# Attention of a fused transformer block, issued by pairs of heads: half-array scores and half-array value products

## The reference, cut to what matters

```python
# layer 0, for each block of 128 queries (12 heads of 64; top keys chosen by an indexer)
s = jnp.einsum('bthd,btkd->bthk', qi, k_sel) * HEAD_DIM ** -0.5
p = masked_softmax(s, valid[:, :, None, :])
out = jnp.einsum('bthk,btkd->bthd', p, v_sel)
# layer 1: three branches (31 compressed keys, selected keys, window), summed with gates
o = gi[..., 0:1] * o_c + gi[..., 1:2] * o_s + gi[..., 2:3] * o_w
# both layers: four more heads over 256 memory keys
s = jnp.einsum('bshd,bnhd->bhsn', q, k) * HEAD_DIM ** -0.5
p = jax.nn.softmax(s, axis=-1)
o = jnp.einsum('bhsn,bnhd->bshd', p, v)
```

## Time and profile before

| what | us |
|---|---|
| median of 3 runs (3523.74 to 3528.39) | 3527.47 |
| the profiled execution's own time | 3527.51 |
| its span in the trace | 3525.7 |
| layer 0's attention, in the trace | 208.6 to 299.3 |
| layer 1's attention, in the trace | 857.8 to 1060.7 |

### The profile page before, as it was taken

How to read it: one execution, slowest core, us unless ns; L and a number is a source line. 1 busy time by engine, 2 the same in 40 slices (tenths; PEclk the granted TensorE clock), 3 DMA queues, 4 the chain that set the end, 5 groups by cost and what they waited for, 6 DMA issues and landing times.

```text
span 3525.7 us, 46614 instructions
## 1 busy us (share of the span) xinstructions
PE 3348.1 (95%) x16902; PEld 2768.0 (79%) x16902; DVE 1657.1 (47%) x2719; ACT 1472.4 (42%) x2771; POOL 1601.7 (45%) x1404
## 2 busy tenths in 40 slices
PE   6899999999999999999989996899999999999998
PEld 4578888877778888788877775788888878888886
DVE  4784433142773332343326876555565552333321
ACT  3355433223664333333325554454445542243322
POOL 4245544662445445544553321444444435464454
PEclk8899999997999999999999997999999999999999
DMA  4111333341002333333332220111111113333332
GB/s 122 42 43 49 95 95 97 94 115 37 1 1 84 95 95 94 95 98 95 94 86 62 59 54 25 37 43 37 42 37 37 39 46 96 96 96 95 98 96 70
DMA packets 471315, 245.93 MB, mean 70 GB/s; under 512 B 13820, under 2 KB 468711, under 8 KB 471015
## 3 DMA queue, kind: packets, MB, share of 16 engines
q1 hardware_dynamic: 470144, 241.33, 24.1%
q10 hardware_dynamic: 998, 2.30, 0.2%
HBM read 241.51 MB, written 2.10 MB: 69 GB/s over the span
## 4 chain that ended last, share of the span: by engine, by line
PE 85%; DVE 8%; ACT 3%; issue 2%; POOL 1%; DMA 0%; ACTq 0%; DVEq 0%; POOLq 0%
PE ps L463 18%; PE ps L464 18%; PE ps L465 18%; PE ps L1545 3%; PE ps L1525 3%; PE ps L2281 2%; PE ps L2177 2%; PE ps L2179 2%; PE ps L2178 2%; PE ps L2263 2%; PE ps L1534 2%; PE ps L1696 1%; PE ps L1697 1%; PE ps L1698 1%; PE ps L1769 1%
## 5 line engine op out<-in xcount | busy, mean ns | idle before, releaser
L445 POOL TENSOR_TENSOR w_lo<-ring,w_hi 128x512 fp32r<-128x512 f32 (+1 forms) x908 | 1223.8, 1369 | 1540.6 <-ACT w_hi L436 1540.6
L436 ACT ACTIVATE w_hi<-ring 128x512 fp32r<-128x512 f32 (+1 forms) x908 | 516.1, 617 | 1276.5 <-PE ps L465 1191.8
L463 PE MATMUL ps<-h_hi,w_hi 128*128 128x512 f32 x1776 | 701.7, 395 | 4.4 <-POOL w_lo L445 4.4
L465 PE MATMUL ps<-h_hi,w_lo 128*128 128x512 f32 x1776 | 691.9, 390 | 0.0
L464 PE MATMUL ps<-h_lo,w_hi 128*128 128x512 f32 x1640 | 638.8, 390 | 0.0
L463 PEld LDWEIGHTS ps<-h_hi,w_hi 128*128 128x128 f32 x1776 | 333.8, 188 | 80.7 <-POOL w_lo L445 6.4
L465 PEld LDWEIGHTS ps<-h_hi,w_lo 128*128 128x128 f32 x1776 | 333.7, 188 | 69.8
L464 PEld LDWEIGHTS ps<-h_lo,w_hi 128*128 128x128 f32 x1640 | 308.4, 188 | 68.5 <-issue 5.0
L464 PE MATMUL ps<-a_lo,w_hi 128*128 128x512 f32 x752 | 292.5, 389 | 0.0
L465 PE MATMUL ps<-a_hi,w_lo 128*128 128x512 f32 x720 | 280.1, 389 | 0.0
L463 PE MATMUL ps<-a_hi,w_hi 128*128 128x512 f32 x720 | 280.1, 389 | 0.0
(11 more groups left out here) (445 smaller groups left out, 6195.1 us busy)
## 6 DMA issues: line engine op xcount, KB each, us to landing
ring<-in_ffn_w_in SPq DMA_DIRECT2D x176, 512.0 KB, 3.8
ring<-in_w_in SPq DMA_DIRECT2D x96, 512.0 KB, 4.0
ring<-in_ffn_w_down SPq DMA_DIRECT2D x32, 512.0 KB, 3.7
ring<-in_ffn_w_out SPq DMA_DIRECT2D x32, 512.0 KB, 3.6
ring<-in_w_o SPq DMA_DIRECT2D x16, 512.0 KB, 3.7
ring<-in_w_branch_gdn SPq DMA_DIRECT2D x16, 512.0 KB, 3.6
ring<-in_nsa_w_in SPq DMA_DIRECT2D x15, 512.0 KB, 3.8
ring<-in_dsa_w_in SPq DMA_DIRECT2D x13, 512.0 KB, 4.1
```

The costliest lines, as they stand in the source:

```text
L436: act.activation(w_hi[:, (halves(u) + j) % PIECES, 0:n, :], slot(u)[:, j * n:(j + 1) * n, :], ACT.Copy) \
L445: pool.tensor_tensor(w_lo[:, q % PIECES, 0:n, :], slot(u)[:, j * n:(j + 1) * n, :], w_hi[:, q % PIECES, 0:n, :].bitcast(f32), ALU.subtract ...
L463: pe.matmul(dst, wh, hi(k), start=first and k == 0, stop=False)
L465: ins = pe.matmul(dst, wl, hi(k), start=False, stop=last and k == 2 * n - 1)
```

## The change

Units are issued two at a time, the two heads of a pair for one query tile and branch (in layer 1 the order becomes tile, branch, head instead of tile, head, branch). The scores contract only the head's own 64 rows, and the value products have 64 weight columns and write only the head's own 64 output partitions, the two heads taking turns for each 128 keys. Each head now has an accumulation of its own. The loops of PE and ACT run over pairs of units: in step i PE issues the scores of both units of pair i, all transposes of pair i-2 and the value products of pair i-3, and ACT both exps of pair i and both evictions of pair i-2. The depths of all buffers and the count of instructions stay.

```diff
-    LEAD = 2
...
-            for t in range(NT):
-                for hh in range(2):
+            for t, br, hh in itertools.product(range(NT), range(1 if i == 0 else 3), range(2)):
...
-                        at = HD * (1 - hh)
+                        at = HD
                         us.append(dict(q=q_rot[:, pair, tok], k=k_dsa[:, hh, 0:nk], bias=bias, nk=nk,
-                                       v=[v_dsa[:, j, at:at + P] for j in range(t + 1)], gate=None, clamp=False,
-                                       out=tok, first=hh == 0, last=hh == 1, pair=pair, need=t))
+                                       v=[v_dsa[:, j, at:at + HD] for j in range(t + 1)], gate=None, clamp=False,
+                                       out=tok, first=True, last=True, pair=pair, need=t))
...
-        for n in range(N + LEAD + LAG_V):
-            if n < N:
-                u = us[n]
-                if n >= 4:
-                    pe.wait_ge(sig("att_masked").sem, t["masked"] + n - 3)
-                pe.matmul(ps[:, SCORE_BANKS[n % 4], 0:u["nk"]], u["q"], u["k"], start=True, stop=True) \
-                  .then_inc(sig("att_scores").sem, 1)
...
+        for i in range(N // 2 + LAG_V):
+            if i < N // 2:
+                if i >= 2:
+                    pe.wait_ge(sig("att_masked").sem, t["masked"] + 2 * i - 2)
+                for n in (2 * i, 2 * i + 1):
+                    u, rows_ = us[n], even_odd[n % 2]
+                    pe.matmul(ps[:, SCORE_BANKS[n % 4], 0:u["nk"]], u["q"][rows_], u["k"][rows_], start=True, stop=True) \
+                      .then_inc(sig("att_scores").sem, 1)
+            s = i - LAG_T
+            if 0 <= s < N // 2:
+                for m in (2 * s, 2 * s + 1):
+                    u = us[m]
+                    pe.wait_ge(sig("att_norm").sem, t["norm"] + m + 1)
+                    if m >= 2:
+                        pe.wait_ge(sig("att_copied").sem, t["copied"] + m - 1)
+                    for at, w in key_tiles(u):
+                        ins = pe.transpose(ps[0:w, 2 + m % 2, at:at + P], pr[:, m % DEEP, at:at + w], ident)
+                    ins.then_inc(sig("att_turned").sem, 1)
+            s = i - LAG_V
+            if 0 <= s < N // 2:
+                pe.wait_ge(sig("att_copied").sem, t["copied"] + 2 * s + 2)
...
                 for j, (at, w) in enumerate(tiles):
-                    ins = pe.matmul(ps[:, 4 + u["pair"] % 2, tok], u["v"][j], prT[0:w, m % 2, at:at + P],
-                                    start=u["first"] and j == 0, stop=u["last"] and j == len(tiles) - 1)
-                ins.then_inc(sig("att_value").sem, 1)
+                    for hh in range(2):
+                        u = us[2 * s + hh]
+                        ins = pe.matmul(ps[even_odd[hh], 4 + u["pair"] % 2, tok], u["v"][j], prT[0:w, hh, at:at + P],
+                                        start=u["first"] and j == 0, stop=u["last"] and j == len(tiles) - 1,
+                                        skip_group_check=True)
...
-            m = n - LAG_V - 2
+            m = n - 2 * LAG_V - 4
...
+        for i in range(N // 2 + LAG_V + 1):
+            if i < N // 2:
+                for n in (2 * i, 2 * i + 1):
+                    u = us[n]
+                    act.wait_ge(sig("att_max").sem, t["max"] + n + 1)
+                    if n >= DEEP:
+                        act.wait_ge(sig("att_turned").sem, t["turned"] + n - DEEP + 1)
...
+            s = i - LAG_T
+            if 0 <= s < N // 2:
+                for m in (2 * s, 2 * s + 1):
+                    u = us[m]
+                    act.wait_ge(sig("att_turned").sem, t["turned"] + m + 1)
+                    if m >= 2:
+                        act.wait_ge(sig("att_value").sem, t["value"] + m - 1)
```

More of the change, by code:

```diff
@@ L8 @@
 import numpy as np
+import itertools
 from concourse import mybir
@@ L1476, in units_of_layer @@
                     g = h // (TOK_HEADS // 2)
[L1477 to L1487, removed]
+                    at = HD * (2 * g + 1)
+                    u = dict(gate=gates[:, t, 3 * h + br:3 * h + br + 1], out=tok, first=br == 0,
+                             last=br == 2, pair=pair, clamp=br == 0, need=0)
+                    if br == 0:
+                        u |= dict(q=q_raw[:, pair, tok], k=k_cmp[:, g, hh, 0:NC], bias=cmp_bias[:, t, 0:NC],
+                                  nk=NC, v=[v_cmp[0:NC, at:at + HD]])
+                    else:
+                        u |= dict(q=q_rot[:, pair, tok], k=k_pad[:, br - 1, g, hh, 0:nk], bias=cb, nk=nk,
+                                  v=[v_tok[:, br - 1, j, at:at + HD] for j in range(t + 1)])
+                    us.append(u)
         for pair in range(MEM_PAIRS):
@@ L1491, in units_of_layer @@
                     tok = slice(t * P, (t + 1) * P)
-                    at = HD * hh
+                    at = 2 * HD * hh
                     us.append(dict(q=q_mem[:, pair, tok], k=k_mem[:, pair, hh, :], bias=const("causal")[:, 0:N_MEM],
-                                   nk=N_MEM, v=[v_mem[:, j, pair, at:at + P] for j in range(MT)], gate=None,
-                                   clamp=False, out=tok, first=hh == 0, last=hh == 1, pair=PAIRS + pair, need=0))
+                                   nk=N_MEM, v=[v_mem[:, j, pair, at:at + HD] for j in range(MT)], gate=None,
+                                   clamp=False, out=tok, first=True, last=True, pair=PAIRS + pair, need=0))
         return us
@@ L1519, in pe_attention @@
         pe.wait_ge(sig("pads_zero").sem, (1, 4)[layer])
-        for n in range(N + LEAD + LAG_V):
-            if n < N:
-                u = us[n]
-                if n >= 4:
-                    pe.wait_ge(sig("att_masked").sem, t["masked"] + n - 3)
-                pe.matmul(ps[:, SCORE_BANKS[n % 4], 0:u["nk"]], u["q"], u["k"], start=True, stop=True) \
-                  .then_inc(sig("att_scores").sem, 1)
[L1527 to L1540, removed]
+        for i in range(N // 2 + LAG_V):
[19 more added lines that the diff above has]
+                pe.wait_ge(sig("att_copied").sem, t["copied"] + 2 * s + 2)
+                u = us[2 * s]
+                if u["pair"] >= 2 and (s == 0 or us[2 * s - 1]["pair"] != u["pair"]):
@@ L1544, in pe_attention @@
                 for j, (at, w) in enumerate(tiles):
[L1545 to L1547 removed]
+                    for hh in range(2):
[3 more added lines that the diff above has]
+                                        skip_group_check=True)
+                        if j == len(tiles) - 1:
+                            ins.then_inc(sig("att_value").sem, 1)
     def dve_attention(dve, ch, t):
@@ L1551, in dve_attention @@
         need = 0
-        for n in range(len(us) + LAG_V + 3):
+        for n in range(len(us) + 2 * LAG_V + 5):
             if n < len(us):
@@ L1590, in act_attention @@
         N = len(us)
[L1591 to L1611, removed]
+        for i in range(N // 2 + LAG_V + 1):
[5 more added lines that the diff above has]
+                        act.wait_ge(sig("att_turned").sem, t["turned"] + n - DEEP + 1)
+                    act.activation(pr[:, n % DEEP, 0:u["nk"]], sm[:, n % DEEP, 0:u["nk"]], ACT.Exp,
+                                   bias=neg_max[:, n % 8:n % 8 + 1], accum_out=row_sum[:, n % 8:n % 8 + 1]) \
+                       .then_inc(sig("att_prob").sem, 1)
+            s = i - LAG_T
[5 more added lines that the diff above has]
+                        act.wait_ge(sig("att_value").sem, t["value"] + m - 1)
+                    w = min(P, u["nk"])
+                    n_t = len(key_tiles(u)) * P
+                    act.activation(prT[0:w, m % 2, 0:n_t], ps[0:w, 2 + m % 2, 0:n_t], ACT.Copy) \
+                       .then_inc(sig("att_copied").sem, 1)
+            m = 2 * (i - LAG_V) - 1
+            if 0 < m < N and (m == N - 1 or us[m + 1]["pair"] != us[m]["pair"]):
```

## The result

The changed kernel takes 3583.86 us (median of 4 runs, 3579.71 to 3592.85) against 3527.93 for the kernel before (4 runs on the same chip): ratio 1.0167, 95% interval 1.0153 to 1.0181. It is slower by 56 us. The forecast was slower by 21.5.

The account below looks back on a forecast made before the run. PE's own issue was taken to bound attention before, a chain through DVE and ACT after. From 3527.5 us, -8 at the full clock and +30 for clock falls gave 3549; own case 3535 to 3565, 8-in-10 range 3516 to 3585.

Parts of the forecast that it names:

- Halves side by side: PE's products on separate array halves overlap: scores fall from 0.43n to 0.21n us per pair-step, value products taken as 0.21n.
- Rival 3: Value products on column halves don't overlap, so hops grow by 0.21c, +27 us: 3566 us; chance 0.15.
- 0.55 us of drains in a pair-step: PE changes array shape three times per pair-step, draining each time: 0.2 + 0.2 + 0.15 us.
- The chain through the second exp and the evictions: From V(i-4) to V(i-2), through scores, both DVE units, second exp, evictions, transposes, values: 1.92 + 0.84a + 0.11b + 0.43c us.
- rival 2: The chain is looser than read and engines' sums decide: 9.5 and 26 us per pair of heads, 3490 us; chance 0.04.
- rival 1: The clock holds in attention, since PE never pauses more than some 3 us: -8, 3519 us, faster; chance 0.15.
- rival 4: The clock stays at 1.2 GHz through attention, PE's sums at half speed, +80 us: 3607 us; chance 0.08.
- rival 5: The clock costs are twice too high and the rest right: 3534 us and below, no measurable change; chance 0.12.
- Both chains have six hops and sizes that add up to 12: ... 28.1: Layer 1's twelve pair-steps per period: 28.1 us against 29.98, -1.9 per pair of heads, -11.4 over six.
- In layer 1 the small steps fall each time, and 3 us ... doubles: +18: Clock falls over layer 1's four small steps each period, doubling 3 us of the chain's PE work: +18 us.
- Layer 0's clock, +5: In layer 0 two of three periods see a clock fall, doubling 1.2 us of PE work: 6 x 0.8 = +5 us.
- The starts: Ramp and tail, one more DVE unit at either end of two layers: +2 us; layer 1's start at half clock: +4.

Follow-up runs that it names:

- half_scores_old_order: The kernel before with only its scores changed to contract the head's own 64 rows, units still issued one by one: 3633.85 us, ratio 1.0294.
- evict_first: The changed kernel with ACT's two evictions of pair i-2 put ahead of its two exps of pair i in each step: 3516.80 us, ratio 0.9971.
- full_scores: The changed kernel with the old scores over all 128 rows, half-array value products kept: 3552.34 us, ratio 1.0077 to the kernel before.

## Why the prediction was right in sign and off in size

- **Halves side by side**: right, for columns too (0.06 us a record). Rival 3 is refuted, though its 3566 was nearer to the time than the forecast.
- **0.55 us of drains in a pair-step**: about right in the sum. The hops of layer 0 at the full clock came out at 5.47 and 6.57 with 5.45 and 6.49 forecast, and the memory step at 2.36 with 2.35 (9.42/4). A single change cost 0.11 to 0.13 us in half_scores_old_order, after what the removed pauses gave, where the sum has 0.15 to 0.2.
- **The chain through the second exp and the evictions**: right, and shown by evict_first and the three like it. It is why PE's saved time didn't show (rival 2 falls with it; rival 1 falls by PEclk, 0.89 and 0.80; rival 4, the clock at half throughout, by PEclk too; rival 5, 3534, by the time). What I held against rival 4, that full stretches bring the clock back, isn't safe either: half_scores_old_order stood at half for 54.5 us with PE busy throughout.
- **"Both chains have six hops and sizes that add up to 12: ... 28.1"**: wrong. I took two chains that don't touch. They share DVE. In layer 0 the even sizes are always the late ones, and the sum holds. In layer 1 equal sizes follow each other, and the path through both chains, as the rows of full_scores have it, is longer than either. full_scores shows 31.5 at the full clock, 1.5 to 2.7 above what was expected of it; the changed kernel's own value, by the slope, is near 30.5. So layer 1 had about nothing to gain even at the full clock (29.98 before): some 2.4 us per pair of heads, 14 us in all, are missing in the forecast.
- **"In layer 1 the small steps fall each time, and 3 us ... doubles: +18"**: the sign right, the size off by about two. Three falls in a period, not one. The mean period of 37.1 us is 6.6 above the 30.5 of the slope and 5.6 above full_scores' period without a fall: 34 to 40 us over six pairs of heads, so 16 to 22 are missing here. I had looked for long pauses only; the falls above stand behind pauses of 1.1 to 1.9 us. I had also counted half-array scores only as PE time saved. With full ones in their place, in the same chain, the time at half clock is 34 us, not 129, and in the old order they brought a fall with no pause in PE's row.
- **Layer 0's clock, +5**: right in its periods (12.9 measured; 11.94 + 0.8 forecast). **The starts**: the first copy comes 8.7 us later in layer 0 and 8.4 in layer 1, of which 2.3 come back between the last token copy and the last memory copy. That makes some 15 us, where the forecast had some 10 for starts, ramps and memory steps.

From copy to copy, layer 1's five periods give +34 where the forecast had 5.5, and that is 28.6 of the 34.5 us by which it missed. The step that failed is thus layer 1's, in two terms, chain and clock. They may feed each other: a slower clock makes the chain's PE work longer, and a longer chain leaves PE more pauses; that the pauses pull the clock is argued, since the half-array scores go with the falls as well. How much is whose stays open within 1 us per period, since no run had the changed kernel's own layer 1 free of falls.

## What to carry to other kernels

Before halving an engine's work, find what it will then wait for. Grouping steps in twos put a second exp between a transpose and its eviction, and cost 50 us; with ACT's two blocks exchanged, the changed kernel's instructions were 0.3% faster than the kernel before. When two chains alternate on the same engines, sum the longest path through both, not each alone: they are independent only if one is always the late one. And TensorE's saved time isn't always free: look at the granted clock, and keep the full-array form where the saving lies off the path (here the scores) and the half-array form only where it lies on it (here the values).

## What the runs showed of the hardware

- Value products on separate column halves of the array, two heads in turn, start every 0.054 us at the full clock, half of the 0.11 of full ones. This is from the changed kernel's layer 0, where 8, 12 and 16 records took 0.59, 0.80 and 1.02 us to the next start (from 245.94, 248.32 and 250.97).
- A change between 64-row scores and full-array work cost 0.11 to 0.13 us each in half_scores_old_order's stream without pauses, after what the removed pauses gave.
- In the changed kernel's layer 1 the clock fell behind stretches in which PE was busy for 38, 44 and 66%, with pauses of 1.1 to 1.9 us in them. Full-array scores in the same chain took the time at half clock in attention from 129 to 34 us.
- It also fell without a pause: in half_scores_old_order PE's row was busy for 150.0 of 150.0 us at the full clock and then for 54.5 of 54.5 at half. With full scores the same order of work shows no such fall. What in the half-array scores does it stays open.
